# Three bfloat16 parts instead of two scaled float16 parts for the gates of a product-key expert layer

## The reference

```python
s = jnp.einsum("nhad,akd->nhak", qh, sub_keys)     # 8 heads, 2 halves, 128 keys
top_s, top_i = lax.top_k(s, 16)
cand = top_s[:, :, 0, :, None] + top_s[:, :, 1, None, :]
best_s, pos = lax.top_k(cand, 16)                  # 16 experts per token and head
eidx = take_along_axis(cand_idx, pos)              # first key * 128 + second key
gate = jax.nn.softmax(best_s, axis=-1)
hpre = einsum("nd,nhkd->nhk", xc, u_tab[eidx])
act = gate * gelu(hpre)
out = einsum("nhk,nhkd->nd", act, v_tab[eidx])
```

## Time and profile before

| | |
|---|---|
| median of three runs | 2041.0 us (2039.93 to 2044.97) |
| profiled execution, its own time | 2039.93 us |
| its span in the trace | 2037.9 us |
| TensorE matmul busy | 1889.6 us, 93% |
| TensorE weight load busy | 1833.0 us, 90% |
| VectorE busy | 1424.0 us, 70% |
| ScalarE busy | 874.7 us, 43% |
| chain that ended last | TensorE 81%, VectorE 14%, ScalarE 3% |
| float32 matmuls L421, L422, L423 | 4336 each, 23%, 22% and 22% of the chain |
| gate matmuls L1492 | 1024, 42.2 us busy |
| L1482, taking the gates | 64, 86.0 us busy |
| L1473, multiplying the one-hots | 128, 54.1 us busy |
| bytes read from memory | 291.67 MB, 144 GB/s over the span |

### The profile page before, as it was taken

How to read it: one execution, slowest core, us unless ns; L and a number is a source line. 1 busy time by engine, 2 the same in 40 slices (tenths; PEclk the granted TensorE clock), 3 DMA queues, 4 the chain that set the end, 5 groups by cost and what they waited for, 6 DMA issues and landing times.

```text
span 2037.9 us, 41749 instructions
## 1 busy us (share of the span) xinstructions
PE 1889.6 (93%) x15336; PEld 1833.0 (90%) x15336; DVE 1424.0 (70%) x2437; ACT 874.7 (43%) x1317; POOL 19.3 (1%) x38
## 2 busy tenths in 40 slices
PE   7979997999799969997789979999999999999997
PEld 7969996988799959986679979999999999999997
DVE  5668886844688863447766549996888889994554
ACT  4333443443343335365444444455444344444443
POOL 0000000010000000000100000000000000000000
PEclk9989997976899989987999989999999999999999
DMA  5525553420455524430026624455444445554553
GB/s 199 185 98 183 181 181 100 156 93 12 164 185 185 182 87 144 135 114 1 1 83 202 200 95 145 165 165 185 166 165 166 164 150 168 167 165 167 176 176 109
DMA packets 80276, 293.70 MB, mean 144 GB/s; under 512 B 8960, under 2 KB 9120, under 8 KB 79824
## 3 DMA queue, kind: packets, MB, share of 16 engines
q1 hardware_dynamic: 79632, 289.96, 43.2%
q0 software_dynamic: 576, 2.79, 0.4%
HBM read 291.67 MB, written 1.05 MB: 144 GB/s over the span
## 4 chain that ended last, share of the span: by engine, by line
PE 81%; DVE 14%; ACT 3%; issue 2%; DMA 0%; DVEq 0%; ACTq 0%
PE ps L421 23%; PE ps L422 22%; PE ps L423 22%; DVE m L395 3%; PE ps L427 3%; PE ps L462 2%; PE ps L1492 1%; DVE m L1394 1%; DVE m L514 1%; PE ps L752 1%; DVE m L1390 1%; ACT m L383 1%; PE ps L751 1%; DVE m L1398 1%; DVE m L508 1%
## 5 line engine op out<-in xcount | busy, mean ns | idle before, releaser
L421 PE MATMUL ps<-m,m 128*128 128x256 f32 x4336 | 1252.7, 289 | 69.2 <-DVE m L522 33.8
L422 PE MATMUL ps<-m,m 128*128 128x256 f32 x4336 | 1235.0, 285 | 0.0
L423 PE MATMUL ps<-m,m 128*128 128x256 f32 x4336 | 1234.4, 285 | 0.0
L395 DVE TENSOR_TENSOR m<-m,m 128x1024 fp32r<-128x1024 f32 x546 | 663.1, 1222 | 432.1 <-ACT m L383 430.5
L421 PEld LDWEIGHTS ps<-m,m 128*128 128x128 f32 x4336 | 840.5, 194 | 83.6 <-issue 53.1
L422 PEld LDWEIGHTS ps<-m,m 128*128 128x128 f32 x4336 | 840.8, 194 | 0.6 <-issue 0.2
L423 PEld LDWEIGHTS ps<-m,m 128*128 128x128 f32 x4336 | 840.0, 194 | 0.0
L383 ACT ACTIVATE m<-m 128x1024 fp32r<-128x1024 f32 x546 | 576.1, 1056 | 472.5 <-PE ps L423 471.1
L1531 ACT ACTIVATE m<-ps 128x256 f32 (+1 forms) x128 | 49.2, 384 | 198.6 <-PE ps L423 198.5
L427 PEld LDWEIGHTS ps<-m,m 128*128 128x128 f32 (+1 forms) x412 | 64.3, 232 | 31.2 <-issue 11.4
L427 PE MATMUL ps<-m,m 128*128 128x128 f32 (+1 forms) x412 | 74.8, 338 | 14.1 <-ACT m L877 10.8
(11 more groups left out here) (198 smaller groups left out, 1131.2 us busy)
## 6 DMA issues: line engine op xcount, KB each, us to landing
m<-stream SPq DMA_DIRECT2D x546, 512.0 KB, 3.3
m<-alibi_t POOLq DMA_DIRECT2D x1, 1536.0 KB, 9.6
m<-con SPq DMA_DIRECT2D x1, 1353.0 KB, 10.1
m<-xT SPq DMA_DIRECT2D x1, 1024.0 KB, 4.9
y<-m SPq DMA_DIRECT2D x4, 256.0 KB, 2.4
m<-wcmpk POOLq DMA_DIRECT2D x1, 512.0 KB, 4.1
m<-wcmpv POOLq DMA_DIRECT2D x1, 512.0 KB, 4.8
m<-par SPq DMA_DIRECT2D x1, 178.0 KB, 5.4
```

What stands on the lines that cost most here:

```text
L395: nc.vector.tensor_tensor(w_lo[:, r, :], raw[:, r, :], w_hi[:, r, :].bitcast(F32), ALU.subtract)\
L421: nc.tensor.matmul(out, lhs[0], rhs[0], start=start, stop=False, **kw)
L422: nc.tensor.matmul(out, lhs[0], rhs[1], start=False, stop=False, **kw)
L423: return nc.tensor.matmul(out, lhs[1], rhs[0], start=False, stop=stop, **kw)
```

## The change

The gates are split into three bfloat16 parts without a scale instead of two float16 parts of the scaled gate. The index, iota and one-hot buffers become bfloat16 too (the same size per element), `gate_part` and `hot_a` get a third part, and `GSCALE` goes.

```diff
-GSCALE = 2.0 ** 14
...
-    gate_full = b_.take(T)
-    gate_part = b_.take(2, T, dt=F16)
+    gate_left = b_.take(1, T)
+    gate_part = b_.take(3, T, dt=BF16)
...
-    hot_b, hot_a = b_.take(GT // 2, P, 2, dt=F16), b_.take(2, GT // 2, HALF, 2, dt=F16)
+    hot_b, hot_a = b_.take(GT // 2, P, 2, dt=BF16), b_.take(3, GT // 2, HALF, 2, dt=BF16)
...
         dc.mark(nc.vector.tensor_tensor(
-            hot_a[:, 1], iota_b[:, half * HALF:half * HALF + HALF, :].unsqueeze(1).broadcast_to(sa),
+            hot_a[:, 2], iota_b[:, half * HALF:half * HALF + HALF, :].unsqueeze(1).broadcast_to(sa),
...
-        for i in range(2):
-            ins = nc.vector.tensor_tensor(hot_a[:, i], hot_a[:, 1],
+        for i in range(3):
+            ins = nc.vector.tensor_tensor(hot_a[:, i], hot_a[:, 2],
                                           pairs(gate_part[:, i, tok]).broadcast_to(sa), ALU.mult)
-            if i == 0:
+            if i == 1:
                 dc.link(ins)
...
-        nc.vector.scalar_tensor_tensor(v, ps[:, 6 + st.mod(2), :].rearrange("p (t a) -> p t a", t=GT), 1.0 / GSCALE, v, ALU.mult, ALU.mult)\
+        nc.vector.tensor_tensor(v, v, ps[:, 6 + st.mod(2), :].rearrange("p (t a) -> p t a", t=GT), ALU.mult)\
...
-            for i in range(2):
+            for i in range(3):
                 ins = nc.tensor.matmul(out, hot_b[:, q // 2, :, q % 2], hot_a[:, i, q // 2, :, q % 2],
-                                       start=i == 0, stop=i == 1)
+                                       start=i == 0, stop=i == 2)
...
-        nc.scalar.activation(gate_full, ps[:, 2, 0:T], ACT.Copy, scale=GSCALE).then_inc(tk_act, 1)
+        nc.scalar.activation(gate_part[:, 0], ps[:, 2, 0:T], ACT.Copy).then_inc(tk_act, 1)
...
-        dc.link(nc.vector.tensor_copy(gate_part[:, 0], gate_full))
-        dc.link(nc.vector.tensor_tensor(gate_part[:, 1], gate_full, gate_part[:, 0], ALU.subtract))
+        dc.link(nc.vector.tensor_tensor(gate_left[:, 0], ps[:, 2, 0:T], gate_part[:, 0], ALU.subtract))
+        dc.link(nc.vector.tensor_copy(gate_part[:, 1], gate_left[:, 0]))
+        dc.link(nc.vector.tensor_tensor(gate_part[:, 2], gate_left[:, 0], gate_part[:, 1], ALU.subtract))
```

More of the change, by code:

```diff
@@ L14 @@
 F32R = mybir.dt.float32r
-F16 = mybir.dt.float16
+BF16 = mybir.dt.bfloat16
 U32 = mybir.dt.uint32
@@ L175, in take @@
             o = self.at
-            size = int(np.prod(dims)) // (2 if dt == F16 else 1)
+            size = int(np.prod(dims)) // (2 if dt == BF16 else 1)
             self.at += (size + 7) // 8 * 8
@@ L278, in build @@
     b_ = Area(O_CONS + COFF["swap"], O_CONS + COFF["rowok"])
-    idx = b_.take(2, T, dt=F16)
-    gate_full = b_.take(T)
-    gate_part = b_.take(2, T, dt=F16)
-    iota_b = b_.take(P, 2, dt=F16)
-    hot_b, hot_a = b_.take(GT // 2, P, 2, dt=F16), b_.take(2, GT // 2, HALF, 2, dt=F16)
+    idx = b_.take(2, T, dt=BF16)
+    gate_left = b_.take(1, T)
+    gate_part = b_.take(3, T, dt=BF16)
+    iota_b = b_.take(P, 2, dt=BF16)
+    hot_b, hot_a = b_.take(GT // 2, P, 2, dt=BF16), b_.take(3, GT // 2, HALF, 2, dt=BF16)
     ez = [(z_hi, z_lo), (at(O_NORM, T, dt=F32R), at(O_NORM + T, T, dt=F32R))]
```

## The result

| | us, median | lowest to highest | runs |
|---|---|---|---|
| before, on the same chip | 2042.99 | 2039.93 to 2049.37 | 4 |
| changed | 2065.84 | 2064.23 to 2066.54 | 4 |
| ratio | 1.0096 | 1.0076 to 1.0115 | |

The kernel became slower, as forecast, but by more: 2065.8 us stand against a forecast of 2055.7 and a range of 2051 to 2062. The profiled execution took 2065.19 us; its span is 2063.1 us, 25.25 more than that of before (2037.9).

What follows compares the result with a forecast made beforehand. TensorE was taken to set the pace in both gate stages: 61 batches x 0.236 = 14.4, plus 0.34, gives 14.7 us. On 2039.93 that is 2054.6, and 1.1 for the runs' median makes 2055.7; range 2051 to 2062.

Steps and rivals of the forecast that it cites:

- the Sum's base: Whole program: profiled execution of 2039.93 us plus 14.7 gives 2054.6; the runs' median of 2041.0 makes it 2055.7.
- +-3 us in all: TensorE restarts behind both hand-overs: half clock loses about 1.5 us each time; whether it recurs is allowed +-3 us.
- The size of the change: Both gate stages and hand-overs: 14.4 us of added matmuls plus 0.34 for the third multiply, 14.7 us.
- 61 x 0.236 = 14.4: Gate batches on TensorE: eight more matmuls at 0.0295 us cost 0.236 a batch, over 61 batches that count.
- VectorE keeps up: Stage two: VectorE needs 6.46 us a batch with the third multiply against TensorE's 6.50, 0.04 to spare.
- The rival in which it takes over: Stage two: VectorE needs 6.66 us a batch and sets the pace, +3.3 us, 2059; chance 11%.
- Taking the gates stays at 1.35 us: L1482 on VectorE: dropping the fused scalar changes nothing, 1354 ns stays; bounds 691 to 1354.
- bfloat16 costs what float16 costs: Gate matmuls and one-hot multiplies: equal width and shape, so 0.0295 us a matmul and 422 ns a multiply.
- The rival of a cheap pair: A batch's 24 gate matmuls: at 0.020 us each they cost what 16 cost, 2041 us, not slower; chance 4%.
- The code stays resident: Gate loop: instruction packets stay near 47; the rival of refetching at each jump would add 16 us, 2072; chance 4%.
- The hand-overs: Behind each stage: the first hides the last batch's 0.24 us; the second adds 0.34 while 0.24 runs beside it.
- Ahead of stage one: Before the first gate batch: VectorE's extra subtraction and multiply, 0.7 us together, stay covered by 1.7 us of slack.

Runs made afterwards that it cites:

- the repeat: The changed kernel run again unedited, beside more runs of the kernel before: 2061.88 us against 2045.89, ratio 1.0078.
- the lifted pair: Kernel before and changed kernel, each with one idle 256-column matmul per head step in both attention stages and filled hand-overs: 2028.07 and 2045.29 us.
- the split run: Kernel before with eight more 64-column float16 matmuls per batch, placed between the two expert chunks: 2068.32 us, ratio 1.0109.

## Why the prediction was right in its direction and wrong in its size

- **The step that failed is the Sum's base**: "The runs' median, 2041.0, is 1.1 above it: 2055.7", with "Whether it falls so again I count as +-3 us in all" for the clock. Three runs were taken for where the kernel stands. 23 more have their median at 2045.9 and go up to 2049.9. From there the forecast's own +14.7 gives 2060.6, near the 2061.9 of the repeat. The miss of 10.1 us (2065.8 against 2055.7) adds up so: 4.9 from the base, 1.3 from the size of the change by medians (16.0 against 14.7), and 4.0 by which the result's four runs lie above the median of the repeat. The last is likely the draw of the clock once more (0.937 to 0.939 in all four), or the chip. That the repeat's 2061.9 lies just inside the range is luck, with a base 4.9 too low. And the clock was reckoned only behind the two hand-overs, where it was worth 1 us in the end, while half clock ahead of the change, 222 us in one profile and 242 in the other, moves the whole program by some 8. The profile's row of PE's clock by slices was there to see; I read it only where the change is. The two profiles of the first comparison lay at opposite ends: before at the low end of its spread, the changed one near the high end of its own.
- **The size of the change** was forecast at 14.7 and is 15.7 (the changed part in two pairs of profiles that keep 2.4 GHz through both hand-overs), 16.0 by the medians of the repeat (18.3 if all twenty runs of the changed kernel count), 16.9 in the first pair of profiles, 17.2 by the medians of the lifted pair. The term mis-sized is "61 x 0.236 = 14.4". The price of one matmul was right (0.0297 to 0.0298 against 0.0295), the batch is longer by 0.24. Missing are the eight turn ends, 0.5 us in all, and the few thousandths by which a batch, longer by 0.240 in stage one and 0.246 in stage two, is above 0.236, another 0.5. The other 1.1 us of the profile is the half clock after the first hand-over, 6.8 us long instead of 3.4 in the changed kernel, its repeat, and the kernels with the third matmul alone, with four, and with one. In the kernels with the third multiply alone, bfloat16 with two parts and the split run it stayed at 3.4. What decides between them stays open.
- **VectorE keeps up**: right, but its count was wrong in two terms, to no effect. The forecast gave it 6.46 us a batch and 0.04 to spare; with the third multiply alone it held 6.27, so 6.46 is too high and the fixed wait of 0.12 in it isn't fixed. In the changed kernel it is idle for 6.8 of 202 us, of which 2.4 before the row multiply: 0.08 a batch, forecast 0.04. The rival in which it takes over is dead: the third matmul alone gives the same stages.
- **Taking the gates stays at 1.35 us**: right. 1356 ns as tensor_tensor, 1354 with the fused scalar, 1350 with two parts. That the 1 KB step between neighbours doubles it rests on the earlier trace rows and on what didn't change; no kernel here took gates into neighbouring elements.
- **bfloat16 costs what float16 costs**: right (421 and 685 ns on VectorE, 97 and 193 on TensorE, ratio 0.9998 for the kernel with two parts). The rival of a cheap pair is dead with it.
- **The code stays resident**: right as far as the packets show, 48 against 47.
- **The hand-overs**: right in the sum. The first hides the last batch (4.89 and 4.90 us), the second costs 0.12 to 0.14 net, forecast 0.10. The forecast made that of +0.34 and -0.24; no run shows the two parts, and the third multiply alone, with no slower TensorE to hide it, cost 0.95 there and not 0.34, so the good sum is in part luck. The 1.5 us put on each slow restart fits the 1.4 and 1.3 that filling the hand-overs saves.
- **Ahead of stage one** the 0.7 us stay covered as far as one can see: TensorE has no stop at the first gate batch. The 8.3 us are clock: four matmuls a token came to the first gate batch at 1426.4, and the third multiply alone at 1434.1.

## What to carry to other kernels

When an engine has no gap left, added instructions cost their start-to-start distance times their count, and the engine beside it gets that time as slack; both could be read from one row each. What could not be read from the changed stages is where the program as a whole stands: before a forecast of under 1%, take the spread from as many runs as there are, and look at the clock row over the whole span, since half-clock stretches in untouched code are worth more than such a change. If such a stretch stands over a stage that keeps TensorE at work all the time, one idle matmul per step is worth a try, there and not in a stage that has 2.4 GHz already.

## What the runs showed of the hardware

- A stage can keep TensorE occupied without a stop (61.40 of 61.40 us) and be granted 1.2 GHz for all of it. One idle 256-column matmul per step gave it 2.4 GHz (a turn of two heads 2.76 us instead of 4.32) and, with the fills at the hand-overs, took 19.5 us off the program and most of its scatter. In a stage at 2.4 GHz the same idle matmul cost 0.22 us. The profile's busy share alone didn't tell which level the stage got. The Trainium skill (TensorE: Matmul & The Clock Gate, section HAM oscillation — how this bites in real kernels) describes a kernel whose clock falls back because it waits for DMA. The trace shows another case: the DMA engines were 1% busy in this stretch, and TensorE's row has no gap in it.
- With stops filled at the norms, one profile has another such stretch, 78.5 us at 1.2 GHz in the second attention stage (2046.7 us), and the profile of the changed kernel with the same fills has none there (2026.4 us). Five more runs of that kernel took 2054 to 2066; that they had the stretch is likely by their mean clock, not shown.
- A run of 24 or 32 short matmuls in front of a loop's jump adds about 0.06 us at the jump; one of 8 or 16 adds none.
- Behind a run of short 16-bit matmuls, of 8 or of 32, the second float32 matmul starts 0.20 us after the first instead of 0.12. A second run of eight in the middle of a batch therefore costs 0.08 us more than eight added to the first.
- An idle of VectorE before an instruction that waits for its forerunner is not fixed: 1.1, 3.7 and 4.3 us in all for 31 batches of almost the same three lines.
